# The opening of a hybrid decoder layer on one core: first loads in halves, transposes of x two units ahead, squares of x spread over five units

## What is computed

```python
def rmsnorm(x, g):
    xf = x.astype(jnp.float32)
    y = xf * lax.rsqrt(jnp.mean(xf * xf, axis=-1, keepdims=True) + EPS)
    return (y * g.astype(jnp.float32)).astype(x.dtype)

h = rmsnorm(x, g_mix_pre[l])
z = h @ w_in[l]
q_lat, c_kv, k_pe, u_pool, gate_a, gate_p = split_cols(z, IN_SIZES)
```

## Time and profile before

| | us |
|---|---|
| median of 3 runs | 1829.41 (1827.87 to 1829.53) |
| the profiled execution, its own time | 1829.66 |
| its span, first to last instruction | 1827.9 |
| TensorE busy (products) | 1810.5, 99% |
| VectorE busy | 1015.9, 56% |
| ScalarE busy | 928.2, 51% |
| GpSimd busy | 60.7, 3% |
| mean granted clock of TensorE | 0.998 |

### The profile page before, as it was taken

One profiled execution on the slowest core, in us unless ns is written; L12 is line 12 of the kernel. 1 busy time (PEld: TensorE's weight loads), 2 busy tenths in 40 slices (PEclk: granted clock), 3 DMA queues, 4 the chain that ended last, 5 costly groups with the idle time before them and its releaser, 6 DMA issues.

```text
span 1827.9 us, 24021 instructions
## 1 busy us (share of the span) xinstructions
PE 1810.5 (99%) x8228; PEld 1481.5 (81%) x8228; DVE 1015.9 (56%) x1416; ACT 928.2 (51%) x1269; POOL 60.7 (3%) x132
## 2 busy tenths in 40 slices
PE   8999999999999999999999999999999999999998
PEld 7888888888888888888888878888888888888886
DVE  5554455555555554544444476666666666744444
ACT  6555556665546554544444464444444444443443
POOL 4000000000000200000000100000000000000000
PEclk9999999999999999999999999999999999999999
DMA  8455544445556655555434555555555555655553
GB/s 281 150 185 179 172 155 155 155 151 178 188 198 216 207 184 184 169 185 192 144 138 164 192 194 187 184 180 177 177 180 182 183 184 178 234 197 192 189 190 109
DMA packets 166408, 330.69 MB, mean 181 GB/s; under 512 B 7846, under 2 KB 13398, under 8 KB 164950
## 3 DMA queue, kind: packets, MB, share of 16 engines
q1 hardware_dynamic: 164806, 318.48, 52.4%
q10 hardware_dynamic: 1552, 11.54, 1.6%
HBM read 325.81 MB, written 4.19 MB: 181 GB/s over the span
## 4 chain that ended last, share of the span: by engine, by line
PE 96%; ACT 2%; issue 1%; DVE 1%; DMA 0%; SPq 0%; DVEq 0%; ACTq 0%
PE bank L454 30%; PE bank L456 30%; PE bank L455 30%; PE bank L842 1%; PE bank L486 1%; PE bank L770 1%; PE bank L787 1%; DMA bufX<-in_x 0%; PE bank L660 0%; PE bank L669 0%; ACT actA L1233 0%; PE bank L653 0%; PE bank L652 0%; ACT L1087 0%; ACT whi L935 0%
## 5 line engine op out<-in xcount | busy, mean ns | idle before, releaser
L1332 DVE TENSOR_TENSOR wlo<-raw,whi 128x1024 fp32r<-128x1024 f32 x612 | 746.6, 1222 | 757.6 <-ACT whi L935 575.5
L935 ACT ACTIVATE whi<-raw 128x1024 fp32r<-128x1024 f32 x448 | 471.1, 1052 | 604.3 <-PE bank L456 604.2
L454 PE MATMUL bank<-whi,actA 128*128 128x512 f32 x1344 | 542.8, 404 | 2.8 <-DVE actA L1632 1.0
L456 PE MATMUL bank<-whi,actA 128*128 128x512 f32 x1344 | 531.3, 395 | 0.0
L455 PE MATMUL bank<-wlo,actA 128*128 128x512 f32 x1344 | 530.7, 395 | 0.0
L454 PEld LDWEIGHTS bank<-whi,actA 128*128 128x128 f32 x1344 | 253.6, 189 | 60.3 <-issue 2.2
L456 PEld LDWEIGHTS bank<-whi,actA 128*128 128x128 f32 x1344 | 253.2, 188 | 59.3
L455 PEld LDWEIGHTS bank<-wlo,actA 128*128 128x128 f32 x1344 | 253.7, 189 | 55.5
L921 ACT ACTIVATE whi<-raw 128x1024 fp32r<-128x1024 f32 (+1 forms) x164 | 168.9, 1031 | 174.6 <-PE bank L456 170.6
L454 PE MATMUL bank<-whi,actB 128*128 128x512 f32 x576 | 229.4, 398 | 0.0
L456 PE MATMUL bank<-whi,actB 128*128 128x512 f32 x576 | 227.3, 395 | 0.0
(11 more groups left out here) (213 smaller groups left out, 1208.3 us busy)
## 6 DMA issues: line engine op xcount, KB each, us to landing
raw<-in_w_ffn_in SPq DMA_DIRECT2D x88, 1024.0 KB
raw<-in_w_in SPq DMA_DIRECT2D x48, 1024.0 KB
raw<-in_w_mem_kv SPq DMA_DIRECT2D x32, 1024.0 KB
raw<-in_w_ffn_out SPq DMA_DIRECT2D x32, 1024.0 KB
raw<-in_w_attn_br SPq DMA_DIRECT2D x16, 1024.0 KB
raw<-in_w_mix_out SPq DMA_DIRECT2D x16, 1024.0 KB
raw<-in_w_mem_q SPq DMA_DIRECT2D x16, 1024.0 KB
raw<-in_w_mem_o SPq DMA_DIRECT2D x16, 1024.0 KB
```

The lines of the kernel that those rows point to most:

```text
L454: pe.matmul(acc[t][:, 0:n], hi, wh, start=f, stop=False)
L456: mm = pe.matmul(acc[t][:, 0:n], lo, wh, start=False, stop=l)
L935: act.activation(whi[:, ks % AHEAD, 0:w], raw[:, c, ks % 2, 0:w], ACT.Copy).then_inc(hi_done, 1)
L1332: dve.tensor_tensor(wlo[:, vs % AHEAD, 0:w], raw[:, c, vs % 2, 0:w], f32(whi[:, vs % AHEAD, 0:w]), ALU.subtract).then_inc(lo_done, 1)
```

## The change

On SP, x's first quarter is loaded as two halves of 256 columns, and slots 0 and 1 as two halves of one unit each, in the order: x half 0, unit 0's weights, x half 1, unit 1's weights, quarter 1, unit 2's, unit 3's, quarter 2, slot 2, quarter 3, slot 3. New semaphores `x_first` and `w_first` announce the first halves. TensorE makes fill 0, six keep-warm transposes, fill 1, six more, and then fill v + 2 after unit v for v = 0 to 5. ScalarE and VectorE order the first steps as split 0, weights 0, split 1, weights 1, weights 2, split 2, weights 3, split 3. In the loop each split k + 4 comes after the weights k + 4, and ScalarE squares pieces 0, 1, (2, 3), (4, 5), (6, 7) at the end of steps 0 to 4. The root stays at k = 5, and VectorE's part of the norm too.

```diff
-        for j, quarters in enumerate(((0,), (1, 2), (3,), ())):
-            for q in quarters:
-                x_quarter(q)
-            load(j, j, w_in[:, 4 * j:4 * j + 4, C_Q:C_Q + NC], NC)
+        def x_half(h, done):
+            o = slice(h * NC // 2, (h + 1) * NC // 2)
+            sp.dma_start(bufX[:, :, o], tok[:, :, o]).then_inc(done, 16)
+
+        def w_half(j, h, done, amount):
+            dst = raw[:, j, h, :].rearrange("p (k n) -> p k n", n=NC)
+            k = 4 * j + 2 * h
+            sp.dma_start(dst, w_in[:, k:k + 2, C_Q:C_Q + NC]).then_inc(done, amount)
+
+        for j in range(4):
+            if j == 0:
+                x_half(0, x_first)
+                w_half(0, 0, w_first[0], 16)
+                x_half(1, x_in[0])
+                w_half(0, 1, w_loaded[0], 32)
+                continue
+            x_quarter(j)
+            if j == 1:
+                w_half(1, 0, w_first[1], 16)
+                w_half(1, 1, w_loaded[1], 32)
+            else:
+                load(j, j, w_in[:, 4 * j:4 * j + 4, C_Q:C_Q + NC], NC)
...
         def x_fill(k):
-            if k % 2 == 0:
+            if k == 0:
+                pe.wait_ge(x_first, 16)
+            elif k == 1 or k % 2 == 0:
                 pe.wait_ge(x_in[k // 2], 16)
             t_fill(T_X + k, k, bufX, 2 * k, four)
 
-        for k in range(4):
-            if k == 2:
-                keep_warm(WARM_UP)
+        for k in range(2):
             x_fill(k)
+            keep_warm(WARM_UP // 2)
...
-            if v < 4:
-                x_fill(v + 4)
+            if v < 6:
+                x_fill(v + 2)
...
-            act.wait_ge(w_loaded[c], 32 * (turn + 1))
+            if v in (0, 2):
+                act.wait_ge(w_first[c], 16)
+            else:
+                act.wait_ge(w_loaded[c], 32 * (turn + 1))
...
-        for k in (0, 2):
-            x_split(k)
-            x_split(k + 1)
+        for k in range(4):
+            if k < 2:
+                x_split(k)
             hi(k, k)
-            hi(k + 1, k + 1)
+            if k >= 2:
+                x_split(k)
         act.wait_ge(part_zero, 1)
+        act.wait_ge(x_first, 16)
         for k in range(16):
-            if k < 4:
-                x_split(k + 4)
             if k % 8 == 7:
                 evac(U_LAT + k // 8, V_LAT + k, [zlat[:, k // 8, t, :] for t in range(TT)], N_X)
             if k == 5:
                 root(N_X)
             hi_at(V_LAT, 0, 16, k)
             if k < 4:
-                act.wait_ge(x_in[k], 16)
-                for t in range(TT):
-                    square(N_X, 2 * k + t, bufX[:, t, k * NC:(k + 1) * NC])
+                x_split(k + 4)
+            if k < 5:
+                for q in ((0,), (1,), (2, 3), (4, 5), (6, 7))[k]:
+                    act.wait_ge(x_in[q // 2], 16)
+                    square(N_X, q, bufX[:, q % 2, q // 2 * NC:(q // 2 + 1) * NC])
```

More of the change, by code:

```diff
@@ L236, in hybrid_layer @@
     x_in = [sem(f"x_in{q}") for q in range(ND)]
+    x_first = sem("x_first")
+    w_first = [sem(f"w_first{c}") for c in range(2)]
     gm_in, g_in, c_in, pos_in = sem("gm_in"), sem("g_in"), sem("c_in"), sem("pos_in")
@@ L1415, in x_split @@
             t_split(T_X + k, k, *tiles(actA, 2 * k), 2 * k, four, gmix)
-        for k in (0, 2):
-            x_split(k)
-            x_split(k + 1)
+        for k in range(4):
+            if k < 2:
+                x_split(k)
             lo(k, k)
-            lo(k + 1, k + 1)
+            if k >= 2:
+                x_split(k)
         for k in range(16):
-            if k < 4:
-                x_split(k + 4)
             if k == 5:
@@ L1427, in _ @@
             lo_at(V_LAT, 0, 16, k)
+            if k < 4:
+                x_split(k + 4)
             if k == 14:
```

## The result

The changed kernel takes 1832.1 us (median of 16 executions, 1830.69 to 1833.61), the kernel before 1828.28 us (median of 16, 1827.87 to 1829.84). The ratio is 1.0019, 95% interval 1.0011 to 1.0026: the changed kernel is slower, by 3.8 us between the medians and 3.5 us by the ratio, and the ratio is just inside the 0.2% that I had called no change. The profiled execution of the changed kernel took 1833.61 us, its span is 1831.8 us, 3.9 us more than the span before.

What follows compares the result with a forecast made beforehand. TensorE, always fed after its first product, bounds the kernel through unit 8's start. Start -2.14, unit 0's clock -1.55, fills and rounding +0.85, stall +3.5, clock +1.55 give +2.2 on 1829.66: 1831.9 us; range 1826.6 to 1833.8.

Steps and rivals of the forecast that it cites:

- What bounds the kernel, and where to look: Whole kernel: TensorE is always fed from its first product, so only unit 8's start, 36.69 us before, matters.
- The start: Opening: with loads in halves, unit 0 starts at 8.8 us, 2.14 earlier; bounds 7.9 and 10.7.
- rival C: Unit 0: transposes in pieces don't hold the clock, so it is low there too, costing 1.55 us: 1833.5; chance 0.13.
- TensorE's path: Unit 0 to unit 8: fill 7 at 27.83, unit 8 could start at 33.85 us, 2.84 before 36.69; landings don't stop it.
- The three more issues on SP: SP's queue: about 0.45 us each, delaying later loads, costed at nothing; 1.4 us without cover.
- rival D: Opening: slot 0's halves land together at 8.27, unit 0 starts at 10.7; 1833.8 us with the stall; chance 0.07.
- ScalarE's chain: Split 7 to unit 8: squares behind split 7 put unit 8 at 37.35 us, 8.8 after its start; TensorE stalls 3.5.
- Rival B: Evacuation before unit 8: ScalarE is in time if its chain is under 5.3 us; 1826.8 us; chance 0.15.
- The clock behind the wait: After the stall at unit 8: the clock falls, costing 1.55 us; bounds 0 and 1.7.
- -1.55 (unit 0's clock): Unit 0: it lasted 4.43 us at a low clock; with shorter gaps the clock stays high, saving 1.55 us.
- two fills and rounding: Between unit 0 and unit 8: six fills instead of four, adding 0.85 us (0.7 and 0.15).

Runs made afterwards that it cites:

- e10: The changed kernel profiled once more, nothing else changed; 1832.27 us.
- e1: The changed kernel with ScalarE squaring two pieces in each of steps 0 to 3; 1831.49 us, ratio 1.0016 to the kernel before.
- e2: The changed kernel with the squares placed where ScalarE waits for weights or fills, written to another bank; 1828.55 us against 1828.56 for the kernel before.
- e3: The changed kernel with one small Sqrt on ScalarE at the start, loading the root's table early; 1831.68 us, ratio 1.0014 to the kernel before.
- e5: The kernel of e2 with the small Sqrt of e3 at the start; 1828.43 us against 1828.17 for the kernel before.
- e8: The kernel of e6 without the twelve keep-warm transposes after fills 0 and 1; 1829.19 us against e6's 1827.30.
- e6: The kernel of e5 with hi 10 after the evacuation instead of before it; 1827.30 us against 1828.17 for the kernel before.
- e7: The kernel before with two more ScalarE activations just before the evacuation of units 0 to 7; 1832.59 us, ratio 1.0027 to the kernel before.
- e9: The kernel before profiled once more, with only an empty line added; 1828.32 us.

## Why the prediction was right, and where it was not

**What bounds the kernel, and where to look.** Right. The difference is made before unit 9; behind it no group of TensorE's waits differs between the two traces by more than 0.4 us.

**The start.** 8.8 us forecast, 9.23 measured. hi 0 was at 6.51 (6.4 forecast); the rest is mostly VectorE's first remainder, which took 1.49 us and not 1.23. e10, e1, e2, e3, e5 and e8 start unit 0 at 9.2 too, while e6's profile shows 8.48, so the start varies by 0.75 us between executions. Unit 0 ran at full rate, and rival C of the prediction fell. e8 shows what the twelve transposes are worth: 1.9 us.

**TensorE's path.** Fill 7 forecast at 27.83, measured 28.28, later by the start's 0.43. The period of 3.23 us held, no landing was in the way, and the halves came apart as loaded, so rival D fell too. The three more issues on SP cost nothing, as assumed: hi 8 (31.09) waits for no landing.

**ScalarE's chain.** The step that decided the case, and it held: 8.8 us forecast from split 7's start to unit 8, 37.68 - 28.91 = 8.77 measured. TensorE idled from 34.3 to 37.68, 3.4 us, where the forecast had 3.5 (the profile lists 3.21, since it counts from the last product's modelled end). e2 and e7 show the cause from both sides: with the squares elsewhere the wait is 0.93 and the time falls by 3.5 us; with the wait alone, and none of the change, the kernel before slows by 4.4. Rival B's threshold was worked out wrongly, though. From split 7's start to the moment when TensorE is free there are 5.3 us (28.55 to 33.85), but the evacuation must start 0.84 us before unit 8 can, so the chain to the evacuation would have to be under 4.5 us, not 5.3. e2 shows it: with no square behind split 7 the chain is 34.58 - 28.91 = 5.67 us, because hi 10 and VectorE's remainder of unit 8 also stand ahead, and TensorE still waits 0.93; in e6, without hi 10 and the table load, it is 4.73 (28.16 to 32.89) and no wait is listed.

**The clock behind the wait.** 1.55 us forecast with bounds of 0 and 1.7. Direction right, and the size that of e10's profile, 1.56 us; but the bounds were too narrow: in the first profile unit 8 takes 2.41 us more than before (5.26 and 2.85). The 16 times of the changed kernel fall in three groups by mean granted clock: five at 1830.7 to 1830.8 us (0.999), nine at 1831.9 to 1832.8 (0.998), two at 1833.2 and 1833.6 (0.997). I had taken one stretch at the lower clock from the earlier trace rows as the longest there is.

**The step that failed** is the term "-1.55 (unit 0's clock)". It is true of the execution profiled and, by times and mean clock, of about one execution in nine; a usual one has no low clock in unit 0 (e9: 2.87 us, 11.25 to 14.12, where the profile I used had 4.43), so there is nothing to save. I noted that the profiled execution (1829.66) lay close to the median of the three shown (1829.41), and two of those three were, by their times, of the rare kind. The forecast time, 1831.9, came out at 1832.1 because the sum was made against that execution, whose own time held the 1.55 us that the sum took off; the forecast difference to it, 2.2 us, is not the 3.8 us between the medians. The other terms, put against the usual execution by e9 and e10, give: unit 0's start 2.0 us earlier (11.25 to 9.25), two fills and rounding 0.8 later, the wait 3.4, the clock 1.56: 3.7 us, against 3.8. Profile against profile, the forecast was 2.2 us and the spans differ by 3.9: unit 8 starts 0.33 us later than forecast (37.68 and 37.35), the low clock costs 2.4 us in unit 8 and 0.2 in the transposes behind it instead of 1.55, and 0.3 lies further on. That the first profile missed by so much and the median did not is in part luck: the profiled execution is the slowest of the 16, and the median falls in the group that the clock term of 1.55 us fits.

**The pages.** That a transpose doesn't count as busy for the clock (the Trainium skill, "TensorE: Matmul & The Clock Gate", Part 4: PE-mode transpose) isn't borne out here: e6 and e8 differ by twelve transposes, all 11 times of e8 are the longer, and in the profiles of e5 and e8 only the one with these transposes has unit 0 at full rate. (These are float32 transposes; the profile lists them as MATMUL and doesn't say in which mode they ran.) Nor does the drain of about 1.38 us beside a table load show (the Trainium skill, "ScalarE: Activation LUTs", What ACT_TABLE_LOAD costs): the load started at 33.57, 0.02 us behind the last reading of a square's sum, took the 1.28 us that the page gives, and the root started at 34.87.

**What stays open.** Why the opening's rate is high early in some executions and not in others, and what decides between the three groups of the changed kernel; the runs show that they exist, not their cause. That the gap of 2.18 us made the clock fall in unit 0 rests on the one profile that has it. That e6 is really faster than the kernel before, by 0.9 us, is likely from the two sets of times, but the ratio's interval includes 1.

## What to carry to other kernels

When work is moved behind something that waits on another engine, add up the whole chain from there to the next point where the bounding engine needs a result, and compare it with that engine's own path; how busy the engine that gets the work is on average (51% here) says nothing. Small work with an early input belongs where its engine waits for data, and what the result doesn't need (here hi 10) belongs behind it. A stall can cost about half as much again through TensorE's clock (1.56 us behind 3.4 us of idling in e10); and before a low clock is booked as a gain, look at the mean clock of several executions, because one profile may be the rare one.

## What the runs showed that I had not expected

The same twelve transposes take 1.47 us in one execution and 2.77 in another, and the execution with the slow ones is the quicker: they bridge the wait for x (e9). After nearly equal waits of 3.1 to 3.2 us the clock stayed at 1.00 in one execution (e7), was low for most of unit 8 in another (e10), and for all of it in a third (the first profile). Shorter waits didn't spare it either: behind 2.35 us unit 8 took 4.25 us (e1, 36.94 to 41.19), behind 2.66 us 5.26 (e3, 37.10 to 42.36); behind 0.93 us it took 2.87 (e2). Removing a table load of 1.28 us gave 0.5 us in one place (e3) and nothing in another (e5), since it ran beside VectorE's part of the norm.
